# Two output projections as seven half-size products each, fewer idle products at the start, and one expert buffer refilled in two halves

## The chip, the core and the metric

The kernel runs on one core of a Trainium2 chip, written by hand against the engines: PE (TensorE, matmuls), DVE (VectorE), ACT (ScalarE), POOL (GpSimd) and SP, which here does nothing but issue DMAs. The engines run their own instruction streams and meet only at semaphores. The metric is the device time of one execution in microseconds (us). All data are fp32. One call of the matmul function in fp32 appears in the trace as two PE records (two passes), so a group of 8 calls is counted as x16 there; a transpose on PE is one record.

## The reference, cut to what matters

A transformer block for 256 tokens with 1024 features. Everything below is in the order in which the kernel does it; `rmsnorm` divides by a root mean square and multiplies by a gain.

```
h = rmsnorm(x, g_mix)
proj = h @ w_in                              # q, k, v, gates of two token mixers
merged = sigmoid(gate_a) * (y_a @ w_up_a) + sigmoid(gate_b) * (y_b @ w_up_b)
x = x + merged @ w_o_mix                     # first output projection, 256x1024 @ 1024x1024
q = rmsnorm(x, g_x) @ w_q_x                  # cross attention with 256 memory rows
x = x + attention(q, k, v) @ w_o_x           # second output projection, 256x1024 @ 1024x1024
logits = rmsnorm(x, g_ffn) @ w_router + b_router
# 32 experts, each token goes to its 4 best:
gu = xb @ w_gu[e] + b_gu[e]                  # 1024 x 2048 weights per expert
y = ((u + 1) * g * sigmoid(1.702 * g)) @ w_down[e] + b_down[e]      # 1024 x 1024 weights
out = rmsnorm(x + sum of gated y, g_final)
```

## The kernel before

**The two halves of the program.** The first part (to about 385 us) computes the mixers, the cross attention and the routing for all 256 tokens. The second part walks over the 32 experts; each has 64 slots for tokens, and its weights are six pieces of 2048 KB (`gu0` to `gu3`, `dn0`, `dn1`), which are read from HBM once and used once.

**Buffers.** `ring` has six slots of 2048 KB. All weights of the first part pass through it in the order of `PIECES`; the SP queue issues a piece as soon as the last PE group that reads the slot's old content has finished (`LAST_USE` names that group, `filled_of` waits for it). The experts' pieces of even experts go to `ring`; odd experts' first five pieces have buffers of their own (`r_odd0` to `r_odd3` and the end of `r_gbx`). In the first part these hold activations: `r_odd1` is `r_tp` (scratch, 1024 KB) and `hT` (1024 KB), `r_odd0` the cross-attention operands and the values. So the odd buffers are loaded in halves, each as its old content dies. SP issues everything in the order in which its program is written, and a wait holds up all that stands behind it. Its last issues before the expert loop (`first_block`, `odd_piece`, `odd_half`) fetch experts 0 and 1; then come `even_heads(1)` and the steady loop, in which SP waits for each buffer's `freed` semaphore. PE raises `freed` after the eight matmul calls that read a `gu` piece.

**The projections.** `sga` holds merged^T and `oxT` the attention output^T (feature chunks of 128 on the partitions: 8 chunks x 256 tokens). The weights lie in two ring slots, `om0`/`ox0` with output columns 0 to 511 and `om1`/`ox1` with 512 to 1023. `project_and_turn` on PE runs four groups (`om0_0`, `om0_1`, `om1_0`, `om1_1`; in the second projection `ro...`): output half n and token tile t, each 8 calls of 128x512 that accumulate over the chunks in one PSUM bank. DVE's `residual` adds each group to `x_tok` (`x_tok` = bank * scale + `x_tok`, one instruction of 128x512). After three groups the first half of x is complete, and PE turns it (8 transposes, `tx0`, `tx1`) ahead of the fourth group; the rest (`tx2`, `tx3`) follows when DVE has added the fourth. DVE's `gained` copies the turned x with its gain into `hT`, the operand of what comes next.

**Rows of the operand.** `begin(name)` waits until the bank that the name gets was drained of its previous user, `end(name)` marks it filled. Banks are dealt in turn over the list of `group_order()`.

**The start.** PE's `keep_busy(bank, n)` issues n products of the identity with itself, whose result nobody reads, in places where PE would be idle: 5 before the gain vector is turned, 4 before x is turned, 3 before the products `rb` that spread the norm's root over a row, and 8 behind `rb`, while ACT and DVE scale the turned x into `hT` for the q projection.

## Time and profile before

| | |
|---|---|
| median of 3 runs | 1299.54 us (1298.63 to 1300.12) |
| the profiled execution's own time, and its span | 1298.83 us, 1297.1 us |
| PE busy | 1244.9 us (96%) |
| DVE busy | 288.7 us (22%) |
| ACT busy | 145.3 us (11%) |
| moved by DMA | 454.70 MB, 351 GB/s over the span |
| mean granted TensorE clock | 0.991 |

The span is the time from the first to the last instruction. A busy PE means that PE had a matmul in flight, which says little by itself: the page's slices show PE busy nearly everywhere, and the DMA engines at 9 tenths or more and 425 to 429 GB/s from the fourteenth of forty slices on (a slice is 32.4 us) to the last but one. In the slices before them the DMA engines carry 85 to 401 GB/s.

### The profile page before, as it was taken

What the parts mean: (1) busy time and instruction counts of PE and PEld (TensorE: products, weight loads), DVE (VectorE), ACT (ScalarE), POOL (GpSimd) and SP (SyncE); (2) the same over time, 40 slices, a digit from 0 to 9 for tenths busy, and PEclk for the clock granted to TensorE, in tenths of its full rate; (3) what the DMA queues carried; (4) which work ended last, traced back from release to release, by engine and by line L of the source; (5) the groups of instructions that cost most, each with busy time, mean ns of one, the idle gap of its engine ahead of it and who ended that gap; (6) DMA issues with size and microseconds to landing.
All of it is one profiled execution on the core that took longest, in us unless ns stands there. A gap on an engine that the chain in (4) does not pass through costs nothing.

```text
span 1297.1 us, 14906 instructions
## 1 busy us (share of the span) xinstructions
PE 1244.9 (96%) x6197; PEld 614.1 (47%) x6197; DVE 288.7 (22%) x697; ACT 145.3 (11%) x325; POOL 8.2 (1%) x34
## 2 busy tenths in 40 slices
PE   9999999999999999999999999999989899999986
PEld 8868886757644343333343333443333344333322
DVE  2362234321132221111121111221111132211112
ACT  2223232101310000000000000000000000000001
POOL 1000000000000000000000000000000000000000
PEclk9999999999999999999999999999999999999998
DMA  9953233357559999999999999999999999999995
GB/s 332 318 194 110 85 131 113 115 195 268 203 195 401 428 428 427 426 427 428 429 429 428 428 429 429 427 428 428 428 428 428 428 428 427 427 427 428 427 425 238
DMA packets 60451, 454.70 MB, mean 351 GB/s; under 512 B 7228, under 2 KB 14072, under 8 KB 35064
## 3 DMA queue, kind: packets, MB, share of 16 engines
q1 hardware_dynamic: 58168, 452.49, 84.9%
q10 hardware_dynamic: 2240, 1.58, 0.4%
q8 instruction: 34, 0.56, 0.2%
q14 instruction: 9, 0.07, 0.0%
HBM read 453.00 MB, written 1.05 MB: 350 GB/s over the span
## 4 chain that ended last, share of the span: by engine, by line
PE 68%; DMA 29%; SPq 1%; issue 1%; DVE 1%; ACT 0%; POOL 0%; DVEq 0%; POOLq 0%; ACTq 0%
PE ps L1331 30%; DMA r_odd<-in_w_gu_dram 17%; PE ps L886 13%; DMA ring<-in_w_down_dram 11%; PE ps L893 7%; PE ps L1308 3%; PE ps L1324 3%; PE ps L1405 2%; PE ps L939 1%; PE ps L1103 1%; PE ps L1432 1%; SPq L494 1%; PE ps L1427 1%; PE ps L905 1%; PE ps L1252 1%
## 5 line engine op out<-in xcount | busy, mean ns | idle before, releaser
L1331 PE MATMUL ps<-r_odd,r_memT 128*64 128x512 f32 x1024 | 226.7, 597 | 15.3 <-DMA r_odd<-in_w_gu_dram 15.2
L1331 PE MATMUL ps<-ring,r_memT 128*64 128x512 f32 x1024 | 225.8, 594 | 11.9 <-DMA ring<-in_w_gu_dram 11.2
L1331 PE MATMUL ps<-ring,r_kx 128*64 128x512 f32 x768 | 176.9, 609 | 11.2 <-DMA ring<-in_w_down_dram 11.2
L1997 DVE TENSOR_SCALAR r_ga<-ps 128x512 f32<-128x512 f32 x32 | 22.1, 692 | 637.6 <-PE ps L1331 637.6
L1331 PEld LDWEIGHTS ps<-r_odd,r_memT 128*64 128x64 f32 x1024 | 73.4, 138 | 166.4 <-issue 137.2
L1331 PEld LDWEIGHTS ps<-ring,r_memT 128*64 128x64 f32 x1024 | 71.8, 137 | 160.2 <-issue 135.7
L886 PE MATMUL ps<-r_odd,ring 128*128 128x256 f32 x576 | 129.5, 383 | 0.0
L886 PEld LDWEIGHTS ps<-r_odd,ring 128*128 128x128 f32 x576 | 109.5, 192 | 18.0 <-issue 3.2
L1331 PEld LDWEIGHTS ps<-ring,r_kx 128*64 128x64 f32 x768 | 54.9, 140 | 130.0 <-issue 108.0
L827 ACT ACTIVATE r_ga<-r_ga 128x512 f32<-128x512 f32 x32 | 20.2, 630 | 462.8 <-DVE r_ga L1997 462.8
L1308 PE MATMUL ps<-r_dm,r_x 128*128 128x128 f32 x512 | 65.8, 282 | 0.0
L1324 PE MATMUL ps<-r_kx,r_dm 64*128 64x512 f32 x256 | 63.6, 615 | 0.7 <-ACT r_kx L833 0.7
L1308 PEld LDWEIGHTS ps<-r_dm,r_x 128*128 128x128 f32 x512 | 62.8, 197 | 1.6 <-DVE r_dm L1927 0.8
L1331 PE MATMUL ps<-r_gbx,r_kx 128*64 128x512 f32 x256 | 58.5, 598 | 0.8 <-DVE r_kx L2010 0.8
L833 ACT ACTIVATE r_kx<-ps 128x512 f32<-128x512 f32 x32 | 19.1, 597 | 333.9 <-PE ps L1331 333.9
L893 PE MATMUL ps<-ring,r_memT 128*128 128x512 f32 x112 | 49.2, 595 | 0.0
L1324 PEld LDWEIGHTS ps<-r_kx,r_dm 64*128 64x128 f32 x256 | 22.0, 186 | 41.3 <-issue 39.7
L1935 DVE TENSOR_TENSOR r_memT<-ps,sm 128x512 f32<-128x512 f32 x32 | 22.1, 692 | 64.6 <-PE ps L1308 64.6
L1331 PEld LDWEIGHTS ps<-r_gbx,r_kx 128*64 128x64 f32 x256 | 16.9, 136 | 40.6 <-issue 27.4
L1405 PE MATMUL ps<-r_ga,r_kx 32*64 32x512 f32 x256 | 35.8, 612 | 0.0
L893 PEld LDWEIGHTS ps<-ring,r_memT 128*128 128x128 f32 x112 | 21.0, 190 | 25.5 <-issue 25.2
L886 PE MATMUL ps<-r_memT,ring 128*128 128x256 f32 x128 | 28.6, 381 | 0.0
(342 smaller groups left out, 804.1 us busy)
## 6 DMA issues: line engine op xcount, KB each, us to landing
ring<-in_w_gu_dram SPq DMA_DIRECT2D x64, 2048.0 KB, 27.9
r_odd<-in_w_gu_dram SPq DMA_DIRECT2D x60, 2048.0 KB, 27.5
ring<-in_w_down_dram SPq DMA_DIRECT2D x47, 2048.0 KB, 22.6
r_gbx<-in_w_down_dram SPq DMA_DIRECT2D x15, 2048.0 KB, 30.2
ring<-in_w_in_dram SPq DMA_DIRECT2D x7, 2048.0 KB, 13.7
r_odd<-in_w_gu_dram SPq DMA_DIRECT2D x8, 1024.0 KB, 13.3
ring<-in_w_k_x_dram SPq DMA_DIRECT2D x2, 2048.0 KB, 9.5
ring<-in_w_v_x_dram SPq DMA_DIRECT2D x2, 2048.0 KB, 7.9
```

What stands on the lines that cost most here:

```text
L494: sp.dma_start(odd_slot[j], gu_dram[e, j] if j < 4 else dn_dram[e, j - 4]).then_inc(odd_loaded[j], 16)
L827: nc.scalar.activation(sig, gact, ACT.Sigmoid, scale=1.702).then_inc(sig_done, 1)
L833: nc.scalar.activation(y_slot, ps[:, ZBK, :], ACT.Copy).then_inc(yslot_ready, 1)
L886: last = mm(o[:, j * T:(j + 1) * T], w(k), src[:, k, :], start=(k == 0), stop=(k == kk - 1))
L893: last = mm(o, src[:, k, t * P:(t + 1) * P], w[:, k, 0:n], start=(k == 0), stop=(k == C - 1))
L905: mm(o[:, 0:P], ident[:], ident[:], start=True, stop=True)
L1308: last = mm(ps[:, buf, c * P:(c + 1) * P], x_rows[:, t, 2 * q + c // 2, c % 2], place[:, t], start=(t == 0), stop=(t == 1))
L1324: last = mm(ps[:, YB + 2 * t + n, :], scat[half, t * P:(t + 1) * P], y_slot[half, :], start=False, stop=False, skip_group_check=True)
L1331: last = mm(ps[n * SLOTS:(n + 1) * SLOTS, bk, :], stationary_, moving(n), start=start, stop=stop, skip_group_check=True)
L1405: mm(ps[n * SLOTS:(n + 1) * SLOTS, GBK + b, :], cur[q * NE:(q + 1) * NE, :], bgu_rows[q * NE:(q + 1) * NE, :], start=True, stop=False, ski ...
L1935: V.tensor_tensor(xg[:, buf, 4 * q:4 * q + 4], ps[:, bank_, :].rearrange("p (c s) -> p c s", c=4), gain_half[q], ALU.mult).then_inc(xg_rea ...
L1997: V.tensor_scalar(gact, ps[:, GBK, :], 7.0, None, ALU.min).then_inc(g_limited, 1)
```

## The change

There are three edits.

**1. Seven products.** Each projection is cut into halves of tokens (rows of the operand), of features (the sum) and of outputs (columns). With operand quarters a11 (tokens 0 to 127, chunks 0 to 3), a12 (tokens 0 to 127, chunks 4 to 7), a21, a22 and weight quarters b11 (chunks 0 to 3, outputs 0 to 511 of `w1`), b21, b12, b22, where `w1` is the slot of `om1`/`ox1` and `w2` that of `om0`/`ox0`, PE computes seven products P1 to P7 of 4 calls each (128x512) in the order of `SEVEN`: 1, 2, 3, 6, 7, 5, 4. DVE makes the sums that they need: four over the operand (128x512, written to `sums`, which is `r_tp`), and four over the weights (128x2048, written in place into the ring slots). DVE adds each product into all quarters of x that it belongs to (`ADDED_TO`: 12 additions of 128x512 in all, in place of 4). `sums_ready` tells PE and DVE how far the sums are.

**2. Idle products.** `keep_busy` is called with 2, 1, 2 and 6 in place of 5, 4, 3 and 8.

**3. First refill in halves.** The first refill of the `gu0` buffer (with the piece of expert 2) is issued as two DMAs of 1024 KB: the first half after PE's first four calls of expert 0 (`first_half_freed`), the second after all eight.

SP's order changes with edit 1: the slot of `om0`/`ox0` is free after P5 and that of `om1`/`ox1` after P4, and the half of `r_odd1` that is `r_tp` is loaded after P5 of the second projection.

```
-            "vx1": "vx3", "ua": "ua3", "ub": "ua3", "om0": "om0_1", "om1": "om1_1", "qx0": "qx1", "qx1": "qx3",
-            "ox0": "ro0_1", "ox1": "ro1_1"}
+            "vx1": "vx3", "ua": "ua3", "ub": "ua3", "om0": "omP5", "om1": "omP4", "qx0": "qx1", "qx1": "qx3",
+            "ox0": "roP5", "ox1": "roP4"}
...
+SEVEN = (1, 2, 3, 6, 7, 5, 4)
+ADDED_TO = {1: ((0, 1), (0, 0), (1, 0), (1, 1)), 2: ((0, 1),), 3: ((0, 0),), 6: ((0, 0), (1, 0), (1, 1)),
+            7: ((1, 0), (1, 1)), 5: ((0, 0), (1, 0)), 4: ((1, 1),)}
...
+            first_block(range(4, 5))
+            filled_of(sp, "roP5")
             odd_half(1, 1, 0)
-            first_block(range(4, 6))
+            first_block(range(5, 6))
...
-            even_heads(1)
+            sp.wait_ge(first_half_freed, 1)
+            sp.dma_start(rows2[:, 0], gu_dram[2, 0][:, 0]).then_inc(first_half_loaded, 16)
+            sp.wait_ge(freed[s], 1)
+            sp.dma_start(rows2[:, 1], gu_dram[2, 0][:, 1]).then_inc(loaded[s], 16)
+            even_heads(1, range(1, HEADS))
...
+                weights(f"{piece_name}1")
+                product(1, upper_left, w1[:, 0:4])
+                product(2, upper_right, w1[:, 4:8])
+                weights(f"{piece_name}0")
+                pe.wait_ge(sums_ready, 5 * turn + 1)
+                product(3, lambda k: sums[:, 3, k], w2[:, 4:8])
+                pe.wait_ge(sums_ready, 5 * turn + 3)
+                product(6, lambda k: sums[:, 1, k], w1[:, 0:4])
+                product(7, lambda k: sums[:, 2, k], w2[:, 0:4])
+                pe.wait_ge(sums_ready, 5 * turn + 4)
+                product(5, lambda k: sums[:, 0, k], w2[:, 4:8])
+                pe.wait_ge(sums_ready, 5 * turn + 5)
+                product(4, lambda k: src[:, 4 + k, P:2 * P], w1[:, 4:8], range(2))
+                drained_of(pe, f"{prefix}P5")
                 transpose4(f"{turned}0", x_tok, 0)
                 transpose4(f"{turned}1", x_tok, 1)
+                product(4, lambda k: src[:, 4 + k, P:2 * P], w1[:, 4:8], range(2, 4))
...
+                link(V.tensor_tensor(sums[:, 0], a21, a22, ALU.add))
+                V.tensor_tensor(sums[:, 2], a11, a21, ALU.subtract)
+                link(V.tensor_tensor(sums[:, 1], sums[:, 0], a11, ALU.subtract))
+                V.tensor_tensor(sums[:, 3], a12, sums[:, 1], ALU.subtract).then_inc(sums_ready, 1)
...
+                V.tensor_tensor(b12, b22, b12, ALU.subtract).then_inc(sums_ready, 1)
...
+                V.tensor_tensor(b11, b12, b11, ALU.add).then_inc(sums_ready, 1)
+                dve.wait_ge(sums_ready, 5 * turn + 3)
+                product_added(1)
+                product_added(2)
+                filled_of(dve, f"{prefix}P3")
+                V.tensor_tensor(b22, b22, b11, ALU.subtract).then_inc(sums_ready, 1)
+                product_added(3)
+                product_added(6)
+                V.tensor_tensor(b21, b21, b11, ALU.subtract).then_inc(sums_ready, 1)
+                product_added(7)
+                product_added(5)
                 gained(f"{turned}0", hT, g0, 0)
                 gained(f"{turned}1", hT, g0, 1)
+                product_added(4)
```

On PE, the first projection stood like this before (`r_ga` is the operand, `ring` the weights, `ps` a bank, the brackets hold the semaphores waited for; `drainedN` is bank N):

```order
L893 MATMUL ps<-ring,r_ga 128x512 [waits merged_ready,drained6,loaded4]
L893 MATMUL ps<-ring,r_ga 128x512 [waits merged_ready] x7
L893 MATMUL ps<-ring,r_ga 128x512 [waits merged_ready,drained7,loaded4]
L893 MATMUL ps<-ring,r_ga 128x512 [waits merged_ready] x7
L893 MATMUL ps<-ring,r_ga 128x512 [waits merged_ready,drained0,loaded5]
L893 MATMUL ps<-ring,r_ga 128x512 [waits merged_ready] x7
L875 MATMUL ps<-ident,r_x 128x128 [waits drained1,drained7,drained6]
L875 MATMUL ps<-ident,r_x 128x128 x3
L875 MATMUL ps<-ident,r_x 128x128 [waits drained2]
L875 MATMUL ps<-ident,r_x 128x128 x3
L893 MATMUL ps<-ring,r_ga 128x512 [waits merged_ready,drained3,loaded5]
L893 MATMUL ps<-ring,r_ga 128x512 [waits merged_ready] x7
```

Now it stands like this from the third product on (ahead of it are P1 and P2, 4 calls each on `r_ga`; `r_odd1` holds the operand sums):

```order
L1218 MATMUL ps<-ring,r_odd1 128x512 [waits drained1,sums_ready]
L1218 MATMUL ps<-ring,r_odd1 128x512 x3
L1218 MATMUL ps<-ring,r_odd1 128x512 [waits drained2]
L1218 MATMUL ps<-ring,r_odd1 128x512 x3
L1218 MATMUL ps<-ring,r_odd1 128x512 [waits drained3,sums_ready]
L1218 MATMUL ps<-ring,r_odd1 128x512 x3
L1218 MATMUL ps<-ring,r_ga 128x512 [waits drained4,sums_ready]
L1218 MATMUL ps<-ring,r_ga 128x512
L891 MATMUL ps<-ident,r_x 128x128 [waits drained5,drained3]
L891 MATMUL ps<-ident,r_x 128x128 x3
L891 MATMUL ps<-ident,r_x 128x128 [waits drained6]
L891 MATMUL ps<-ident,r_x 128x128 x3
```

Two calls of P4 stand ahead of the 8 transposes and two behind them, and the transposes wait for bank 3, P5's. Three of the seven products wait for `sums_ready` by themselves, and P6's wait covers P7.

On DVE, the same projection before (`ps` to `r_x` is one addition into x, `ps,vT` one turned pair of chunks):

```order
L1833 SCALAR_TENSOR_TENSOR r_x<-ps,r_x 128x512 [waits filled6,x_again]
L1833 SCALAR_TENSOR_TENSOR r_x<-ps,r_x 128x512 [waits filled7]
L1833 SCALAR_TENSOR_TENSOR r_x<-ps,r_x 128x512 [waits filled0]
L1569 TENSOR_TENSOR r_odd1<-ps,vT 128x512 [waits filled1]
L1569 TENSOR_TENSOR r_odd1<-ps,vT 128x512 [waits filled2]
L1833 SCALAR_TENSOR_TENSOR r_x<-ps,r_x 128x512 [waits filled3]
L1569 TENSOR_TENSOR r_odd1<-ps,vT 128x512 [waits filled4]
L1569 TENSOR_TENSOR r_odd1<-ps,vT 128x512 [waits filled5]
```

Now, from the third operand sum on (the first two stand ahead of it; `ring<-ring` is a sum over weights):

```order
L1887 TENSOR_TENSOR r_odd1<-r_odd1,r_ga 128x512
L1888 TENSOR_TENSOR r_odd1<-r_ga,r_odd1 128x512 [waits v_chain]
L1891 TENSOR_TENSOR ring<-ring 128x2048 [waits loaded5,loaded4]
L1894 TENSOR_TENSOR ring<-ring 128x2048 [waits filled6,sums_ready]
L1881 SCALAR_TENSOR_TENSOR r_x<-ps,r_x 128x512 [waits filled6,sums_ready]
L1881 SCALAR_TENSOR_TENSOR r_x<-ps,r_x 128x512 x3
L1881 SCALAR_TENSOR_TENSOR r_x<-ps,r_x 128x512 [waits filled7,drained6]
L1899 TENSOR_TENSOR ring<-ring 128x2048 [waits filled0,drained7]
L1881 SCALAR_TENSOR_TENSOR r_x<-ps,r_x 128x512 [waits filled0]
L1881 SCALAR_TENSOR_TENSOR r_x<-ps,r_x 128x512 [waits filled1,drained0]
L1881 SCALAR_TENSOR_TENSOR r_x<-ps,r_x 128x512 x2
L1902 TENSOR_TENSOR ring<-ring 128x2048 [waits drained1]
```

The first weight sums stand ahead of every addition, and P1 is added four times before the sum for P5 is made.

On SP, the last issues before the expert loop were these (`filledN` is bank N filled by PE, `freedN` a ring slot that PE has finished with):

```order
L491 DMA r_odd0<-in_w_gu_dram 128x2048 [waits filled5]
L491 DMA r_odd1<-in_w_gu_dram 128x2048
L483 DMA ring<-in_w_down_dram 128x4096 [waits filled7]
L483 DMA ring<-in_w_down_dram 128x4096 [waits filled3]
L491 DMA r_odd2<-in_w_gu_dram 128x2048 [waits sq_done]
L491 DMA r_odd1<-in_w_gu_dram 128x2048 [waits filled5]
L483 DMA ring<-in_w_gu_dram 128x4096 [waits freed4]
L483 DMA ring<-in_w_gu_dram 128x4096 [waits freed5]
```

Now they are these:

```order
L500 DMA r_odd0<-in_w_gu_dram 128x2048 [waits filled0]
L492 DMA ring<-in_w_down_dram 128x4096 [waits filled6]
L500 DMA r_odd1<-in_w_gu_dram 128x2048 [waits filled6]
L492 DMA ring<-in_w_down_dram 128x4096 [waits filled7]
L500 DMA r_odd2<-in_w_gu_dram 128x2048 [waits sq_done]
L500 DMA r_odd1<-in_w_gu_dram 128x2048 [waits filled5]
L549 DMA ring<-in_w_gu_dram 128x2048 [waits first_half_freed]
L551 DMA ring<-in_w_gu_dram 128x2048 [waits freed4]
L492 DMA ring<-in_w_gu_dram 128x4096 [waits freed5]
```

The half of `r_odd1` has moved behind the first `dn` piece and its wait, and the first refill is two rows in place of one.

## Rows read from the trace of the kernel before

**Rows 1.** Waits of PE, whole span: waiter, releaser, us in total, times, longest.

```profile
PE ps L1331 <- DMA r_odd<-in_w_gu_dram: 15.2, 11, 2.3
PE ps L1331 <- DMA ring<-in_w_down_dram: 11.2, 6, 2.7
```

**Rows 2.** Windows: stretch, length, engines busy, PEclk, DMA share, GB/s (last).

```profile
383.00:384.00 1.00, 1.00 (x11) 0.88 (x11) 0.00 (x0) 0.00 (x0) 0.00 (x0) 1.00 0.06 25
389.50:390.00 0.50, 0.50 (x6) 0.50 (x6) 0.00 (x0) 0.00 (x0) 0.00 (x0) 1.00 2.48 459
...
395.50:396.00 0.50, 0.50 (x6) 0.14 (x2) 0.00 (x0) 0.00 (x0) 0.00 (x0) 1.00 1.51 393
600.00:1200.00 600.00, 572.51 (x2894) 221.05 (x2892) 112.18 (x258) 34.05 (x64) 0.00 (x0) 0.99 1.01 428
```

**Rows 3.** Chain of waits, second projection to first expert: start, us, what.

```profile
342.43 20.60 PE ps L893 x48
363.03 0.87 PE ps L875 x8
363.90 6.88 PE ps L893 x16
...
384.98 3.58 PE ps L1331 x16
388.57 2.08 PE ps L1308 x16
390.65 9.59 PE ps L1331 x43
```

**Rows 4.** Chain of waits, first projection.

```profile
269.33 20.60 PE ps L893 x48
```

**Rows 5.** Timeline of DVE around the first projection: start, us, instruction [idle before].

```profile
270.09 0.69 DVE L1826 TENSOR_TENSOR r_ga<-r_ga,r_gbx 128x512 f32<-128x512 f32 x1
...
290.57 1.28 DVE L1569 TENSOR_TENSOR r_odd<-ps,vT 128x512 f32<-128x512 f32 x2
```

**Rows 6.** Groups of DVE by form: line, operands, count, busy us, mean ns.

```profile
L1666 DVE TENSOR_TENSOR r_odd<-r_odd 128x1024 f32<-128x1024 f32 x1 | 1.2, 1226 | 0.0
```

**Rows 7.** Timeline of SP's DMA queue from the second projection on.

```profile
356.19 14.94 SPq L483 DMA_DIRECT2D ring<-in_w_down_dram  x2
...
388.61 12.86 SPq L483 DMA_DIRECT2D ring<-in_w_gu_dram  x4
```

**Rows 8.** DMA issues of the page: KB each, us from issue to landing.

```profile
ring<-in_w_gu_dram SPq DMA_DIRECT2D x64, 2048.0 KB, 27.9
```

**Rows 9.** Chain of waits, the first microseconds.

```profile
2.15 2.50 PE ps L905 x10
...
6.86 2.42 PE ps L918 x16
...
9.95 0.45 PE ps L926 x4
10.40 1.79 PE ps L905 x16
```

**Rows 10.** Timeline of the first microseconds, all engines.

```profile
4.12 1.06 ACT L679 ACTIVATE r_odd<-r_x 128x1024 f32<-128x1024 f32 x1 [1.20 <-DMA r_x<-in_x_dram]
...
4.58 0.27 PE L910 MATMUL ps<-ident,r_odd 8*128 8x8 f32 x1
...
5.46 1.23 DVE L1577 SCALAR_TENSOR_TENSOR r_odd<-r_x 128x1024 f32<-128x1024 f32 x1 [5.46 <-DMA r_x<-in_x_dram]
...
7.24 0.17 DVE L1585 RECIPROCAL sm<-sm 128x2 f32<-128x2 f32 x1 [0.27 <-ACT sm L681]
...
10.93 3.23 DVE L1591 SCALAR_TENSOR_TENSOR r_odd<-ps,vT,r_dm 128x256 f32<-128x256 f32 x8 [3.52 <-ACT r_dm L669]
...
12.02 13.98 PE L939 MATMUL ps<-r_odd,ring 128*128 128x256 f32 x64
```

**Rows 11.** Window of PE at the first gate projections: PE busy, PEclk, DMA, GB/s.

```profile
87.00:88.00 1.00, 1.00 (x3) 0.50 0.88 326
```

More of the change, by code:

```diff
@@ L107, in group_order @@
         g += [f"ub{n}", f"ua{n}"]
[L108 removed]
+    g += [f"omP{n}" for n in SEVEN] + ["tx0", "tx1", "tx2", "tx3"]
     g += ["qx0", "qx1", "sx0", "qx2", "sx1", "qx3", "sx2", "pt0", "sx3"]
@@ L112, in group_order @@
     g += [f"ox{HX - 1}"]
-    g += ["ro0_0", "ro0_1", "ro1_0", "tf0", "tf1", "ro1_1", "tf2", "tf3"]
+    g += [f"roP{n}" for n in SEVEN] + ["tf0", "tf1", "tf2", "tf3"]
     return g
@@ L255, in program @@
         wr = r_kx[:, 1536:1536 + C * NE].rearrange("p (c e) -> p c e", c=C)
+        sums = r_tp.rearrange("p (s k t) -> p s k t", s=4, k=4)
         nar4 = r_p[:, 512:768]
@@ L1193, in _, with project_and_turn, product, upper_left @@
                 end(f"ua{n}", feature_group(f"ua{n}", [stationary(w, 2 * n), stationary(w, 2 * n + 1)], yaT, PAIRS))
-            def token_group(prefix, piece_name, src, n, t, ready):
-                weights(f"{piece_name}{n}")
-                name = f"{prefix}{n}_{t}"
-                end(name, token_part(begin(name), wslot(f"{piece_name}{n}", C, 512), 512, src, t, ready))
-            def project_and_turn(prefix, piece_name, src, turned, ready):
-                token_group(prefix, piece_name, src, 0, 0, ready)
-                token_group(prefix, piece_name, src, 0, 1, ready)
-                token_group(prefix, piece_name, src, 1, 0, ready)
-                drained_of(pe, f"{prefix}0_0")
-                drained_of(pe, f"{prefix}0_1")
+            def project_and_turn(prefix, piece_name, src, turned, ready, turn):
+                w1, w2 = wslot(f"{piece_name}1", C, 512), wslot(f"{piece_name}0", C, 512)
+                def product(n, lhs, rhs, part=range(4)):
+                    o = begin(f"{prefix}P{n}") if part[0] == 0 else bank(f"{prefix}P{n}")
+                    for k in part:
+                        last = mm(o, lhs(k), rhs[:, k], start=(k == 0), stop=(k == 3), skip_group_check=True)
+                    if part[-1] == 3:
+                        end(f"{prefix}P{n}", last)
+                def upper_left(k):
+                    ready(k)
+                    return src[:, k, 0:P]
+                def upper_right(k):
+                    ready(4 + k)
+                    return src[:, 4 + k, 0:P]
+                weights(f"{piece_name}1")
[12 more added lines that the diff above has]
+                drained_of(pe, f"{prefix}P5")
@@ L1421, in gate_up @@
                                 last.then_inc(gate_done, 1)
+                        if is_block(i, 0) and kk == 0:
+                            last.then_inc(first_half_freed, 1)
                     last.then_inc(odd_freed[j] if odd and j < HEADS else freed[eslot[EXPERT_PIECES[j]]], 1)
@@ L1827, in _, with residual_and_turned, product_added @@
                     .then_inc(merged_ready, 1)
-            def residual(prefix, n, t, scale):
-                name = f"{prefix}{n}_{t}"
-                filled_of(dve, name)
-                xv = x_tok[:, t, n * 512:(n + 1) * 512]
-                drain(name, V.scalar_tensor_tensor(out=xv, in0=bank(name), scalar=scale, in1=xv, op0=ALU.mult,
-                                                   op1=ALU.add))
-            def residual_and_turned(prefix, scale, turned, g0):
-                for n, t in ((0, 0), (0, 1), (1, 0)):
-                    residual(prefix, n, t, scale)
+            def residual_and_turned(prefix, piece_name, src, scale, turned, g0, turn):
+                w1, w2 = wslot(f"{piece_name}1", C, 512), wslot(f"{piece_name}0", C, 512)
+                b11, b21, b12, b22 = w1[:, 0:4], w1[:, 4:8], w2[:, 0:4], w2[:, 4:8]
+                a11, a12, a21, a22 = (src[:, k:k + 4, t:t + P] for t in (0, P) for k in (0, 4))
+                def product_added(n):
+                    name = f"{prefix}P{n}"
+                    filled_of(dve, name)
+                    for t, half in ADDED_TO[n]:
+                        xv = x_tok[:, t, half * 512:(half + 1) * 512]
+                        last = V.scalar_tensor_tensor(out=xv, in0=bank(name), scalar=scale, in1=xv, op0=ALU.mult, op1=ALU.add)
+                    drain(name, last)
+                    drained_of(dve, name)
+                link(V.tensor_tensor(sums[:, 0], a21, a22, ALU.add))
+                V.tensor_tensor(sums[:, 2], a11, a21, ALU.subtract)
+                link(V.tensor_tensor(sums[:, 1], sums[:, 0], a11, ALU.subtract))
+                V.tensor_tensor(sums[:, 3], a12, sums[:, 1], ALU.subtract).then_inc(sums_ready, 1)
+                for slot in (f"{piece_name}0", f"{piece_name}1"):
+                    dve.wait_ge(loaded[slot_of[slot]], need[slot])
+                V.tensor_tensor(b12, b22, b12, ALU.subtract).then_inc(sums_ready, 1)
+                dve.wait_ge(sums_ready, 5 * turn + 2)
+                filled_of(dve, f"{prefix}P1")
+                V.tensor_tensor(b11, b12, b11, ALU.add).then_inc(sums_ready, 1)
[9 more added lines that the diff above has]
+                product_added(5)
```

32 lines of the change are left out of this document (18 added, 14 removed).

## The prediction

> **What bounds the kernel now.** I read PE's waits first. The two largest are for weights of experts, 26.4 us over 17 waits, and the third of PE's rows is of the same kind [rows 1]. From 600 to 1200 us the DMA engines are full at 428 GB/s while PE is busy 572.5 of 600 us [rows 2]. So in the expert part the stream of weights sets the end. Its length is fixed by bytes, and what can move the end is when the stream starts without a gap.
>
> Then the windows around its start. At 383 to 384 us the engines are almost idle (25 GB/s): experts 0 and 1 have been fetched as far as buffers allow. SP's next issue, at 388.61 us, is the first refill [rows 7], and data flow from 389.5 us [rows 2]. It is released by the first eight calls of expert 0 (sixteen records, 3.58 us, from 384.98 us) [rows 3]. So the stream starts when PE gets there, and DMA had been idle for some 6 us before.
>
> Last, the chain of waits over the first part: it is PE nearly throughout. The projections stand in it whole: 48 records in 20.60 us, 8 transposes in 0.87 us, 16 records in 6.88 us [rows 3], and the same 20.60 us in the first projection [rows 4]. Hence a microsecond that PE saves before 385 us should come off the end, until the prefetch of experts 0 and 1 is no longer done in time.
>
> **The change part by part.**
>
> *Seven products, PE side.* One record of 128x512 takes 20.60/48 = 0.429 us, one call 0.858 us. A projection had 32 calls and now has 28. Four calls less are 3.43 us; two projections give **6.87 us**, if PE waits for nothing new. The transposes stay.
>
> *Seven products, DVE side.* This is what could take it back. Prices: an addition or an operand sum of 128x512 takes 0.69 us [rows 5]. A weight sum is 128x2048 fp32 from two tensors in SBUF. No row shows that size; 128x1024 takes 1.226 us [rows 6], so each 512 columns above the first 512 add 0.534 us, and 2048 columns take 2.29 us. Independent instructions of 128x512 overlap: two took 1.28 us [rows 5], so 0.6 us each but the last; for one that waits for another I add 0.05 us. The bound from below is this 2.29 us; from above I take four instructions of 128x512, 2.77 us. I take 2.29, since the size step is read from the same operation.
>
> Clock starts at P1 = 0 (269.33 us) [rows 4]. DVE has merged the last chunks at 270.09 + 0.69, that is 1.45. PE without waits ends P1, P2, P3, P6, P7, P5 at 3.4, 6.9, 10.3, 13.7, 17.2, 20.6 and half of P4 at 22.3.
> - Four operand sums: 4.3. PE wants them for P3 at 6.9.
> - Weight sums b12 and b11: 6.5 and 8.8. PE wants b11 for P6 at 10.3, a slack of 1.5.
> - P1 added four times, 11.4; P2 once, 12.1; b22, 14.5. P5 wants it at 17.2, a slack of 2.7.
> - P3 once, P6 three times, 17.1; b21, 19.4. P4 wants it at 20.6, a slack of 1.2.
> - P7 twice, 20.7; P5, filled at 20.7, twice, 22.05. The transposes want it at 22.3, a slack of 0.3.
>
> So PE never waits, and DVE, busy some 19 of the 22 us, is just not the bound. The tail behind P4 is as before: one addition, then two times four transposes. The x that DVE adds to was read again long before, since in the trace DVE's first addition waits for PE alone. With 2.77 us per weight sum the chain ends at 24.0 and the transposes lose 1.7 us per projection. In the second projection the operand is copied out by ACT instead of merged by DVE, 0.6 us behind PE's end, so DVE starts 0.8 us earlier against PE and the slacks grow by it.
>
> *DMA order.* P5's slot is released at 20.6 after the projection's start, P4's at 24.9; before, it was 13.8 and 28.4 (356.19 us is 13.8 behind 342.43) [rows 3, 7]. In the second projection this puts a 2048 KB piece and the 1024 KB half of `r_odd1` at 20.6, a piece at 24.9, and two more halves. That is 7.3 MB behind 20.6, at 428 GB/s 17.2 us, plus about 1 us from issue to first data (388.61 to 389.5) [rows 2, 7]: the engines are done at 38.8 and idle again. The first half refill is issued by the eight records (1.79 us) after PE starts expert 0, which stood at 384.98 - 342.43 = 42.55 and now at 39.1, so at 40.9. The prefetch is done with 2 us to spare, and the saving is passed on. Gaps of this kind ahead of the first projection are larger.
>
> *Refill in halves.* The first 1024 KB start 1.79 us earlier. But the next piece's buffer is released only at 390.65 + 3.58 = 394.2 us, since PE makes a gather between the two (2.08 us) [rows 3], and its data could flow from about 395.1 us. The first piece needs 4.9 us at full rate (2048 KB) [rows 8] and in fact filled 389.5 to about 395.5 us [rows 2]. So before, it overran the second piece's start by 0.4 us at most; finishing it earlier buys that and leaves a gap. Bounds 0 and 0.7 us; I take **0.2**.
>
> *Idle products.* PE starts at 2.15 us and its ten records take 2.50 us, 0.25 each, while the sixteen behind `rb` take 1.79, 0.112 each [rows 9]: TensorE runs at 1.2 GHz first and at 2.4 GHz later, and the transposes of x (16 in 2.42 us) [rows 9] hold the step; at 0.23 and 0.11 each it lies near 8.1 us. x's first tile is there at 4.12 us and its second at 5.46, the root at 7.41, while PE gets to the transposes at 6.86 and to `rb` at 9.95 [rows 9, 10]. So PE's idle products are late for x by 2 us. After the change: two products to 3.15, the gain's transpose (done at 4.58 before, its DMA unseen), one product, transposes from 4.12, eight at 0.23 to 6.0, eight to 7.8, two products to 8.5, `rb` (0.45 us) to 8.95 instead of 10.40. What follows (0.53 us of ACT to DVE's start at 10.93, 1.09 us to the q projection at 12.02) is the same, and six products (1.34 us) fit in it. Gain 1.45 us; if the gain vector lands only at 4.58 it is 0.75. I take **1.3**. From 12 us on PE is fed by weights that came earlier than it needs them, and waits for none up to the experts (its largest waits are those of [rows 1]).
>
> **Sum.** 6.87 + 0.2 + 1.3 = 8.4 us, against the profiled execution's 1298.83 us: 1290.4 us. That execution lies 0.7 us under the median of the three runs, so 1291 us on the median's scale (0.65% less). A difference of 0.2%, 2.6 us, is about what a measurement of this kernel can tell.
>
> **The rivals.**
>
> *A. Forecast*, PE's saving passes to the end: 1291 us. Chance 0.60. Its own range is 1289 (start 1.8, halves 0.7) to 1293.
>
> *B. The clock rises later.* Ahead of 8.1 us PE would now have done three idle products and mostly transposes, before it did nine. If the step comes only behind the q projection's start, transposes end at 7.8, two products at 8.8, `rb` at 9.7, six products at 0.5 us each at 12.7: q starts 0.7 us later than before, and each us of it at the lower level costs half. With 0 to 2.4 us of that the start loses 0.7 to 1.9 instead of gaining 1.3: 1293 to 1294.2 us. For it speaks that at 87 to 88 us the granted clock is 0.50 with PE busy 1.00 of 1.00 us [rows 11], so a busy PE alone does not settle it. Against it, that the step before came in the midst of transposes. Chance 0.17. The Trainium skill, TensorE: Matmul & The Clock Gate, Part 4: PE-mode transpose, says that transposes do not count as activity for the clock the way products do; by that rule this case is the likelier, and the time would be some 1293.5 us. The trace agrees only in part, since the clock there rose during transposes. The stretch at 87 us may shift as well, and each microsecond of it at the lower level is worth half of one, either way.
>
> *C. DVE is just too slow*: sums at 2.77 us, or 0.1 us more for each of its twenty instructions. PE then waits 1.7 us ahead of each pair of transposes: 1294.4 us. Chance 0.10.
>
> *D. Slower: weight sums crawl.* They read and write the ring slots from which PE streams at the same time, which nothing in the kernel before does. At twice the price (4.6 us each) PE waits 3.1 us at P6, 1.1 at P5, 3.8 at P4 and 1 at the transposes; each projection takes 33.9 us up to its last addition instead of 28.4, and the time is 1309 us. It decides from 1.1 us more per weight sum (3.4 instead of 2.3), where a projection loses what the start gains. DVE and PE do run side by side on SBUF all along at unchanged durations, which speaks against it. Chance 0.05.
>
> *E. The saving is not passed on*: the prefetch, now later in SP's order, is still running when the first refill is due. At 351 GB/s, the mean of the span, 7.3 MB take 20.9 us and end 1.6 us late; at 270 GB/s they end 7.9 us late: 1293 to 1299 us. Chance 0.08, as the engines hold 428 whenever they have work.
>
> The two edits beside the products may also do nothing: then 1292.5 us, inside A's range.
>
> **How the numbers follow.** A and B together hold 0.77; the range 1288.7 to 1295.5 takes in them and C. Faster by over 0.2% means under 1296.9: A, B, C and a little of E, 0.88. Within 0.2%: half of E and the edge of C, 0.07. Slower: D, 0.05.
>
> **What the profile after would show.** Right: 56 calls in place of 64 in the projections, each from P1 to the last addition in about 25 us; DVE's 128x2048 at 2.29 us; no wait of PE for DVE over 0.3 us in them; the q projection from about 10.7 us; SP's first refill at about 378.5 us with DMA idle ahead of it; the last record of PE 8.4 us earlier. Wrong would be a PE wait at P6 or the transposes (C, D), 0.25 us products behind `rb` (B), or DMA busy without a gap through 378 us (E).

## The result, and the profile after

| | before | after |
|---|---|---|
| median, range | 1299.28 us (1295.21 to 1300.12, 5 runs) | 1287.30 us (1286.96 to 1290.66, 5 runs) |
| profiled execution's own time, its span | 1298.83, 1297.1 us | 1287.77, 1286.0 us |
| mean granted clock | 0.991 | 0.995 |

The ratio is 0.9918, with a 95% interval of 0.9899 to 0.9938. The forecast was 1291.0 us, in a range of 1288.7 to 1295.5. So the change is faster, as forecast, but by 12 us where 8.4 were expected, and the time lies 1.4 us below the range. The spans differ by 11.1 us, and later runs of both kernels side by side (experiment 10) had medians 11.3 us apart, so some 0.7 us of the 12 is scatter between sets of runs. The rows of after that answer to the groups before the prediction show where the 11.1 us come from.

The chain of waits of after, first microseconds (start, us, what); [rows 9] are those of before:

```profile
0.78 3.83 DMA r_x<-in_x_dram
...
4.66 3.08 PE ps L934 x16
...
8.19 0.51 PE ps L942 x4
...
9.21 0.89 DVE r_odd L1632 x2
...
10.23 14.05 PE ps L955 x64
```

The norm's products (the x4 that ends at 8.70 us) start at 8.19 us, where it was 9.95 us, and the q projection at 10.23 instead of 12.19 us. In the chain stands x's DMA now, not PE's idle products.

The same view around the two projections and the first expert; [rows 3, 4] are those of before:

```profile
267.65 22.32 PE ps L1218 x52
289.97 0.87 PE ps L891 x8
290.84 1.73 PE ps L1218 x4
```

```profile
337.35 22.32 PE ps L1218 x52
...
376.47 3.58 PE ps L1368 x16
380.06 2.08 PE ps L1345 x16
```

52 records in 22.32 us are 0.429 us each, as before, so no wait lies among them. Records and transposes of a projection are 22.32 + 0.87 + 1.73 = 24.92 us, where they were 20.60 + 0.87 + 6.88 = 28.35: 3.43 us less in each.

DVE in the first projection (timeline; in brackets the idle time ahead), the answer to [rows 5, 6]:

```profile
269.21 0.69 DVE L1885 TENSOR_TENSOR r_odd<-r_ga 128x512 f32<-128x512 f32 x1
...
271.87 2.28 DVE L1891 TENSOR_TENSOR ring<-ring 128x2048 f32<-128x2048 f32 x1
274.19 2.29 DVE L1894 TENSOR_TENSOR ring<-ring 128x2048 f32<-128x2048 f32 x1
...
286.82 1.28 DVE L1881 SCALAR_TENSOR_TENSOR r_x<-ps,r_x 128x512 f32<-128x512 f32 x2
288.36 1.29 DVE L1881 SCALAR_TENSOR_TENSOR r_x<-ps,r_x 128x512 f32<-128x512 f32 x2 [0.26 <-PE ps L1218]
```

A weight sum of 128x2048 takes 2.28 to 2.29 us. From the first operand sum to the additions of P5 DVE is idle once, 0.26 us for PE's P5, and it is not late. It adds into x 14 times in each projection (5, 4, 2, 2 and 1 in its timeline), not 12 times as the section on the change says; the prediction's chain counts them rightly. PE's new rows in that section begin at P6, the fourth product (bank 1), and not at P3.

SP's queue and windows of after (PE busy, PEclk, DMA share and GB/s at the end), the answer to [rows 2, 7]:

```profile
378.38 0.33 SPq L549 DMA_DIRECT2D ring<-in_w_gu_dram  x1
380.10 0.33 SPq L551 DMA_DIRECT2D ring<-in_w_gu_dram  x1
385.76 7.19 SPq L492 DMA_DIRECT2D ring<-in_w_gu_dram  x3
400.31 3.76 SPq L492 DMA_DIRECT2D ring<-in_w_down_dram  x2
```

```profile
377.00:378.00 1.00, 1.00 (x8) 0.32 (x6) 0.00 (x0) 0.00 (x0) 0.00 (x0) 1.00 0.14 41
378.00:379.00 1.00, 1.00 (x6) 0.29 (x4) 0.00 (x0) 0.00 (x0) 0.00 (x0) 1.00 0.02 8
385.00:386.00 1.00, 1.00 (x8) 0.30 (x6) 0.00 (x0) 0.00 (x0) 0.00 (x0) 1.00 0.45 188
387.00:388.00 1.00, 1.00 (x8) 0.29 (x4) 0.00 (x0) 0.00 (x0) 0.00 (x0) 1.00 0.40 106
400.00:402.00 2.00, 2.00 (x12) 0.72 (x10) 0.00 (x0) 0.00 (x0) 0.00 (x0) 1.00 1.03 442
402.00:404.00 2.00, 2.00 (x12) 0.61 (x10) 0.00 (x0) 0.25 (x1) 0.00 (x0) 1.00 0.94 393
```

The first refill is issued at 378.38 us, behind a gap in which DMA moved 8 to 41 GB/s. A second gap lies at 385 to 388 us, ahead of the issue of gu1's refill at 385.76 us.

**The end.** SP's queue (timeline), and of the DMA view from 1275 us on the row of instruction fetches (packets, MB, share) and the output's issues (KB each, median us to landing), of after:

```profile
1281.40 2.51 SPq L602 DMA_DIRECT2D out_dram<-r_x  x4
```

```profile
q8 instruction: 1, 0.02, 0.3%
...
out_dram<-r_x SPq DMA_DIRECT2D x4, 256.0 KB, 2.0
```

and of a repeated run of the kernel before (experiment 1), whose end is the same as before's:

```profile
1287.42 3.80 SPq L585 DMA_DIRECT2D out_dram<-r_x  x4
```

```profile
q8 instruction: 2, 0.03, 0.7%
...
out_dram<-r_x SPq DMA_DIRECT2D x4, 256.0 KB, 3.2
```

The four output DMAs took SP 2.51 us after and 3.80 us before. In the trace three of them take 0.33 to 0.36 us each in both, and the fourth 0.33 us after and 1.63 us before. It also lands later. With the longer issue goes one more transfer of the kind "instruction", 16384 B, in the last 5 us.

**Where 11.1 us are.** Worked out from the two traces, each stretch from the start of one group to the start of the next, in us:

| stretch | before | after | gained | predicted |
|---|---|---|---|---|
| to the q projection | 12.19 | 10.23 | 1.96 | 1.3 |
| to P1 of the first projection | 257.14 | 257.42 | -0.28 | 0 |
| two projections, to the last addition | 28.38, 28.38 | 24.95, 24.95 | 6.86 | 6.87 |
| between them and on to expert 0 | 58.89 | 58.92 | -0.03 | 0 |
| expert 0 to the last scatter products | 901.79 | 901.18 | 0.61 | 0.2 |
| last scatter products to the end | 10.33 | 8.35 | 1.98 | 0 |

### The profile page after: what moved, and what is told of

Read it like the earlier page. It is cut to its first block, busy times and chain, and to the rows that moved or that the text cites. A ratio compares the mean times of both kernels' runs of the same rounds, so it can differ in the third digit from the quotient of the medians.

```text
span 1286.0 us, 14893 instructions
## 1 busy us (share of the span) xinstructions
PE 1233.1 (96%) x6163; PEld 607.7 (47%) x6163; DVE 324.7 (25%) x733; ACT 145.2 (11%) x325; POOL 8.0 (1%) x34
## 4 chain that ended last, share of the span: by engine, by line
PE 67%; DMA 30%; SPq 1%; DVE 1%; issue 1%; ACT 0%; DVEq 0%; ACTq 0%
PE ps L1368 30%; DMA r_odd<-in_w_gu_dram 18%; PE ps L902 13%; DMA ring<-in_w_down_dram 12%; PE ps L1218 4%; PE ps L909 3%; PE ps L1345 3%; PE ps L1361 3%; PE ps L1442 2%; PE ps L955 1%; PE ps L1119 1%; PE ps L1473 1%; SPq L503 1%; PE ps L1468 1%; PE ps L1289 1%
## 5 line engine op out<-in xcount | busy, mean ns | idle before, releaser
L1218 PE MATMUL ps<-ring,r_odd 128*128 128x512 f32 x64 | 27.8, 592 | 0.0
L902 PEld LDWEIGHTS ps<-r_memT,ring 128*128 128x128 f32 x128 | 24.0, 190 | 4.2 <-issue 1.0
## 6 DMA issues: line engine op xcount, KB each, us to landing
ring<-in_w_k_x_dram SPq DMA_DIRECT2D x2, 2048.0 KB, 10.6
```

What stands on the lines that cost most here:

```text
L902: last = mm(o[:, j * T:(j + 1) * T], w(k), src[:, k, :], start=(k == 0), stop=(k == kk - 1))
L1218: last = mm(o, lhs(k), rhs[:, k], start=(k == 0), stop=(k == 3), skip_group_check=True)
```

## The experiments

Each kernel was run with a profile and then in rounds against the kernel before. "The end" below is the last row of the table, from the start of the last scatter products to the end of the span. The first is a repeat, and the three behind it split the change into its edits.

**1. The kernel before once more.** No edit.

> The kernel before once more, for the spread. Theory T (tail by chance): in the two first profiles the program from the last matmul to the end took 8.3 us before and 6.4 us after, because the issue of the last output DMA took 1.63 us in the one and 0.36 in the other; if that is chance, this profile may show either, and the time is 1296 to 1300 us. Theory L (layout): the long issue belongs to the place of the instruction in SP's program, so it is there again at 1.6 us and the time is 1299 us.

1299.42 us (11 runs, 1295.71 to 1299.66), ratio 1.0004 (0.9996 to 1.0013). The profiled execution was one of the few near 1295: span 1294.0. The clock rose at 5.66 us instead of 8.12, the q projection began at 11.00 us, and the group of 64 records at 86 us took 14.01 us where before's took 15.38 with a fall of the clock in it. The spans differ by 3.1 us, of which these two make 2.6, and no edit made them. The end was 10.34 us, with the fourth issue at 1.63 us again.

**2. Only the start** (2, 1, 2, 6 in place of 5, 4, 3, 8).

```
-            keep_busy(bank("q1"), 5)
+            keep_busy(bank("q1"), 2)
...
```

> Only the counts of idle products (2, 1, 2, 6 in place of 5, 4, 3, 8). The start theory: q projection at 10.2 us, first expert at 383.3 us, 1.7 us less in all. Rival: the shift of the later fall of the clock (at 87 us) takes it back, 0 to 1 us less. If the tail theory L holds, the last issue is as long as before, since SP's program is the same; if T, it may be short.

1294.26 us (12 runs), ratio 0.9972 (0.9963 to 0.9981), some 4 us (2.5 to 4.8 by the ratio) where 1.3 were predicted for it. In the trace the q projection began at 10.19 us, 2.0 us earlier, and the end took 8.40 us, 1.9 us less. So an edit in the first 10 us took 2 us off the last 10. The two spans differ by 2.3 us only, since the stretch from expert 0 to the last scatter products took 903.10 us here and 901.79 in before. Theory L, as put for these first runs (the long issue belongs to its place in SP's program), fell: SP's program is the same, and the long issue is gone.

**3. Only the refill in halves.**

```
-            even_heads(1)
+            sp.wait_ge(first_half_freed, 1)
+            sp.dma_start(rows2[:, 0], gu_dram[2, 0][:, 0]).then_inc(first_half_loaded, 16)
...
```

> Only the first refill of gu0 in two halves. The sum of the prediction: 0.2 us less, bounds 0 and 0.7. Rival: the 0.6 us by which the expert stream gained beyond the start of expert 0 is this edit's, 0.6 us less. Under L the tail may be 1.3 us shorter too, since SP's program is one DMA longer; then 1.9 us less in all.

1299.06 us (11 runs), ratio 0.9999 (0.9990 to 1.0007). It is worth nothing that can be measured. The end was 10.33 us, so one DMA more in SP's program did not shorten it either.

**4. Only the seven products** (idle products 5, 4, 3, 8 as before, one refill).

> Only the seven products with the order of SP that belongs to them. PE theory: each projection 3.43 us less to its last addition (24.9 in place of 28.3), expert 0 at 378.1 us, and 6.9 us less in all, 1292.4 us. Rival: the products gave more than PE's four calls (for instance by SP's new order of prefetch), 8 us or more less. Under L the tail is as before or 1.3 us shorter, depending on the place.

1289.46 us (5 runs), ratio 0.9922 (0.9910 to 0.9935). From P1 of the first projection to expert 0 it took 108.83 us (270.28 to 379.11), where before took 115.65: 6.82 us less. The end took 8.39 us. Expert 0 came at 379.11 us and not at the 378.1 expected, since the clock fell for 6.8 us near 85 us, and the group of 64 records there took 16.34 us, 1 us more than before's 15.38.

After these the end was long (10.3 us) in three traces and short (8.4) in three, and the short ones were those with fewer calls in PE's stream. The next runs ask whether that is chance.

**5. Four calls fewer on PE.** The kernel before with 5, 4, 3, 4.

> The kernel before with 4 idle products in place of 8 behind the norm's products: PE's stream is 4 calls shorter, nothing else changes. Numbers so far: from the start of the last scatter products to the end of the span it took 10.33 to 10.34 us in three traces of kernels whose PE stream is as long as before, and 8.35 to 8.40 us in three whose stream is 8, 9 and 17 calls shorter; the fourth output DMA's issue took 1.63 to 1.70 us in the first and 0.36 us in the second. Theory L (where a fetch of instructions falls at the end depends on the length of PE's stream): with a boundary somewhere between 0 and 8 calls less, this run decides on which side of 4 calls it lies; with a short end the median is 2 us under the kernel before (1297.4), with a long one the same. Theory T (it is chance): either, and no tie to the length. Start: the q projection begins when DVE has its operand, so 4 idle products less cost nothing (12.2 us again) unless the clock falls or rises elsewhere.

1298.95 us (10 runs), ratio 1.0007 (0.9997 to 1.0018). The end was long, 9.87 us, with two fetches:

```profile
1291.39 3.37 SPq L585 DMA_DIRECT2D out_dram<-r_x  x4
```

```profile
q8 instruction: 2, 0.03, 0.5%
```

The q projection began at 11.32 us and not at the 12.2 expected, but expert 0 only at 386.05, 1.1 us later than in before: the clock fell for 6.8 us, and the group of 64 records near 86 us took 16.43 us.

**6. Idle products moved, not removed.** 2, 1, 2, 15, as many as before.

> The kernel before with its 20 idle products placed 2, 1, 2 and 15 in place of 5, 4, 3 and 8: PE's stream is as long as before, but x is turned as early as in the changed kernel. Theory L (length of PE's stream): the end is long again, 10.3 us, with the fourth output DMA's issue at 1.6 us. Theory T (chance): short or long. Theory of the start (PE was late for x): the norm's products come 1.5 us earlier; the 15 products then take 1.7 us in place of 0.7 for the 6 of the changed kernel, and the q projection begins at about 10.8 us instead of 10.2, which is 1.4 us before the 12.2 us of the kernel before. In all a gain of 1.4 us: 1298.0 us. If what helps is only that PE has fewer products in all, the q projection begins at 12 us and there is no gain.

1299.87 us (10 runs), ratio 1.0013 (1.0004 to 1.0023). The end was long, 10.26 us, as the length theory has it. The start's expectation was wrong. Its chain of waits:

```profile
4.69 3.40 PE ps L918 x16
...
8.98 3.35 PE ps L905 x30
12.33 13.82 PE ps L939 x64
```

x was turned as early as in the changed kernel, and the norm's products were done at 8.98 us. But 15 idle products are 30 records, 3.35 us (I had priced 15 records), and the q projection waits behind them until 12.33 us. What the idle products in front of x win can be lost behind `rb`. Here too the clock fell for 6.8 us, and the group near 86 us took 16.50 us.

**7. A longer PE stream.** The changed kernel with 160 waits that are long fulfilled.

```
+            for _ in range(160):
+                pe.wait_ge(consts, 1)
             four_blocks(6, 0)
```

> The changed kernel with 160 waits on a semaphore that was raised in the first 2 us, ahead of the block of expert 24 in PE's stream: 80 instructions more, which puts the length of PE's stream above that of the kernel before (in instructions, at four for each fp32 matmul call, the changed kernel has 64 less). Nothing is computed differently. Theory L: the end becomes long, 10.3 us in place of 8.35, the fourth output DMA's issue 1.6 us in place of 0.36, and the median is about 2 us over that of the changed kernel, 1289.3. Theory T: the end stays as it falls out, with no tie to the length. Rival: the waits themselves cost time. They stand where PE has about 5 per cent of slack against the stream of weights; at 0.05 us each they take 4 us there, which that slack would absorb; if not, the last expert moves by up to 4 us and the end stays at 8.35.

1288.83 us (4 runs), ratio 0.9928 (0.9911 to 0.9945), 1.5 us over the changed kernel's 1287.30, where 2 were expected. PE was held 4.7 us at the waits, but the stretch from expert 0 to the last scatter products took 901.68 us, 0.5 more than in after. The end took 10.52 us, 2.2 more. Expert 0 had begun 1.3 us earlier than in after, as the clock did not fall near 86 us. SP's queue and the DMA queues there:

```profile
1280.63 4.02 SPq L602 DMA_DIRECT2D out_dram<-r_x  x4
```

```profile
q8 instruction: 2, 0.03, 0.7%
...
out_dram<-r_x SPq DMA_DIRECT2D x4, 256.0 KB, 3.4
```

The second fetch and the long issue are back, with nothing added but instructions of PE.

**8. Seven calls fewer on PE.** The kernel before with 5, 4, 3, 1, three calls less than experiment 5.

> The kernel before with one idle product behind the norm's products in place of 8: PE's stream is 7 calls (28 instructions) shorter than before, as short as that of the kernel with the seven products alone. With 16 instructions less the end was still long (9.9 us, two instruction fetches), with 28 less by other means it was 8.4 us with one. Theory L (length of PE's stream): the end is 8.4 us here, the fourth output DMA's issue 0.36 us. Without it: 9.9 to 10.3 us. Start: DVE's operand sets the q projection, as with 4 idle products (11.3 us), not the idle products (12.2 us before). The median would be 1 us for the start and 2 us for the end under the kernel before, 1295.5 us; if the clock falls or rises later for want of products, the start loses up to 1 us.

1296.70 us (10 runs), ratio 0.9987 (0.9974 to 0.9999). The end took 8.42 us, with one fetch:

```profile
1291.34 2.50 SPq L585 DMA_DIRECT2D out_dram<-r_x  x4
```

```profile
q8 instruction: 1, 0.02, 0.3%
```

So the end is as theory L has it. The q projection began at 11.28 us, set by DVE's operand (11.32 in experiment 5). The median is 1.6 us under the kernel before's in these rounds (1298.31), and not the 3 us expected: the clock fell for 6.8 us again, the group near 86 us took 16.39 us, and expert 0 began at 386.00 us.

**9. DVE's margin.** The changed kernel with three more operand sums on DVE.

```
+                for _ in range(3):
+                    link(V.tensor_tensor(sums[:, 0], a21, a22, ALU.add))
                 link(V.tensor_tensor(sums[:, 0], a21, a22, ALU.add))
```

> The changed kernel with three more sums of 128x512 on DVE ahead of the first operand sum of each projection, each waiting for the one before: 3 x 0.65 = 2 us more work for DVE ahead of everything it does there. The prediction gave slacks of 1.5 us at P6, 2.7 at P5, 1.2 at P4 and 0.3 at the transposes. If these were right, PE now waits 0.5 us at P6, in all 0.8 at P4 and in all 1.7 at the transposes, in each projection: the projections take 26.6 us instead of 24.9, and the time is 3.4 us over the changed kernel's, some 1290.7. If DVE in truth had more room (1 us at the transposes), it is 2 us over. If the waits added up instead of taking each other's place (0.5 + 0.8 + 1.7 each), it would be 6 us over.

1290.63 us (4 runs), ratio 0.9944 (0.9926 to 0.9961). PE's waits in the first projection:

```profile
PE ps L1218 <- DVE ring L1896: 0.8, 1, 0.8
PE ps L891 <- DVE r_x L1881: 0.5, 1, 0.5
```

The three sums took 2.14 us. From P1 to the transposes the first projection took 24.16 us and the second 23.29, in place of 22.31. So the first lost 1.85 us of the 2.14, a margin of 0.3, and the second 0.98, a margin of 1.2. The prediction had 0.3 and 1.1. Behind these the waits took each other's place and did not add up. Together that is 2.8 us, where I had reckoned with 3.4 and left the second projection's extra margin out. That the median lies 3.3 us over the changed kernel's 1287.30, next to the 3.4, is in part luck.

**10. The changed kernel once more.** No edit.

> The changed kernel once more, beside the other three of this call. 1287.3 us (1287.0 to 1290.7) as before; the end from the last scatter products on 8.35 us, with one instruction fetch in it; the projections 22.3 us from P1 to the transposes. The q projection begins at 10.2 to 11.2 us, with the step of the granted clock (7.0 to 9.0 us in the three traces with these idle products).

1287.04 us (5 runs, 1286.37 to 1287.53), ratio 0.9917 (0.9903 to 0.9932). The clock rose at 8.75 us, the q projection began at 11.04, and the clock did not fall in the group near 86 us (14.01 us against after's 15.70). The end took 8.40 us.

**11. The second refill in halves too.**

```
+            for j in range(2):
+                s = eslot[f"gu{j}"]
...
+                sp.wait_ge(first_half_freed, j + 1)
+                sp.dma_start(rows2[:, 0], gu_dram[2, j][:, 0]).then_inc(half_loaded[j], 16)
...
-            even_heads(1, range(1, HEADS))
+            even_heads(1, range(2, HEADS))
```

> The changed kernel with the second refill (gu1 of expert 2) in two halves like the first. In its trace DMA moved 426 GB/s up to 377 us, 8 to 131 at 378 to 380, and again only 188, 254, 106 and 262 at 385 to 389, ahead of the issue of gu1's refill at 385.76 us; from 389 on it is full. Theory G (the last gap sets the start of the stream, and the first refill in halves gave nothing because this gap stays behind it): the first half of gu1's refill is now issued 1.79 us earlier, at 383.97 us, the data of 385 to 389 are about 0.9 MB more, and the end comes up to 1.8 us earlier: 1285.6 us. Theory N (the end is not tied to these bytes, or the next buffer, free 3.6 us later, makes a gap of its own): nothing, 1287.3 us.

1287.44 us (5 runs), ratio 0.9917 (0.9903 to 0.9931): no gain over experiment 10. The gap did close. Windows of the same stretches as above:

```profile
385.00:386.00 1.00, 1.00 (x6) 0.29 (x4) 0.00 (x0) 0.00 (x0) 0.00 (x0) 1.00 1.03 385
387.00:388.00 1.00, 1.00 (x8) 0.34 (x6) 0.00 (x0) 0.00 (x0) 0.00 (x0) 1.00 1.05 426
400.00:402.00 2.00, 2.00 (x12) 0.69 (x10) 0.00 (x0) 0.00 (x0) 0.00 (x0) 1.00 1.03 360
402.00:404.00 2.00, 2.00 (x12) 0.60 (x10) 0.00 (x0) 0.18 (x1) 0.00 (x0) 1.00 0.88 344
```

At 385 to 388 us DMA now moves 385 to 426 GB/s where it moved 106 to 188. But at 400 to 404 it moves 360 and 344, where after has 442 and 393: the lead ends at the next buffers, which SP refills at 400.38 us, as before at 400.31, when PE is done with them. Counted over SP's queue from the start of expert 0, 378.1 MB were left after 12 us against after's 378.9, and 371.2 in both after 30 us. Theory G fell, and N holds.

**12. No idle products at all.** The changed kernel with 0, 0, 0, 0.

> The changed kernel with no idle products at all. Up to 7.9 us PE then does one transpose of the gain and the 16 records that turn x. Theory B (the clock rises later for want of products): the granted clock rises behind 9.0 us, the latest of the traces so far, the transposes of x take 3.7 us in place of 3.1, and the q projection, 64 records of 0.22 us, loses half a microsecond for each one at the lower clock: it begins at 10.5 and ends up to 2 us later than in the changed kernel, 1289 us. Theory A (idle products do nothing for the clock's step): it rises between 5.7 and 9.0 us as in all the traces so far, the norm's products begin 0.3 us earlier with the root, and the q projection at 9.9 to 10.9 us: 1287.0 us.

1285.33 us (4 runs, 1284.98 to 1287.49), ratio 0.9910 (0.9892 to 0.9928). The chain of waits at the start:

```profile
4.58 3.65 PE ps L934 x16
8.23 0.47 PE ps L942 x4
...
9.21 0.89 DVE r_odd L1632 x2
...
10.23 14.05 PE ps L955 x64
```

The clock rose at 8.07 us, inside the 5.66 to 9.04 of all other traces, and the q projection began at 10.23 us. Theory B fell in this trace, and the median is 3.7 us under the 1289 that it gave. Of all kernels here this had the lowest median, 1.7 us under that of experiment 10, which ran beside it. 0.8 us of that is the start (10.23 against 11.04), and 0.8 the stretch from expert 0 to the last scatter products (900.21 against 901.01). Neither trace has a fall of the clock near 86 us. With 4 and 5 runs whose ranges overlap, the two are not told apart.

## Why the prediction was right, and where it failed

**The step that failed is the sum's silent assumption that the saving passes to the end one for one, with nothing changed behind the experts' last products (a term of 0 without a reason).** Expert 0 did move by 384.98 - 376.47 = 8.51 us. A further 2.0 us came off the end: 1.29 us of SP's fourth issue and 0.7 us of its landing. Without them the median would have been 1289.3 us, inside the range. The end over PE's stream length, counted in the programs against the kernel before (an fp32 call is four instructions, two PE and two weight-load records):

| kernel | PE's stream | fetches of 16384 B from 1275 us on | the end, us |
|---|---|---|---|
| after_waits | +16 | 2 | 10.52 |
| before, before_again, halves_alone, moved | 0 | 2 | 10.33, 10.34, 10.33, 10.26 |
| last_four | -16 | 2 | 9.87 |
| seven_less, seven_alone | -28 | 1 | 8.42, 8.39 |
| start_alone | -36 | 1 | 8.40 |
| after, after_again, sums_more, gu1_halves | -64 (gu1_halves -63) | 1 | 8.35, 8.40, 8.37, 8.33 |
| no_idle | -107 | 1 | 8.35 |

Fourteen traces split without an exception, and two pairs that differ in PE's stream alone flip it: last_four and seven_less (12 instructions), after and after_waits (80). That the length of PE's stream decides is shown for these lengths, from +16 to -107; where the switch lies between -16 and -28, and whether it comes back further off, is not. The trace does not name the engine whose instructions are fetched. It does show how closely the issue is tied to the fetch. In all six traces with a second fetch, SP's fourth issue begins 0.14 to 0.45 us behind the start of the fetch and ends 0.37 to 0.38 us behind its end, and without a fetch this issue takes 0.33 us. So the issue stands until the fetch is over; in last_four, where the fetch took 0.95 us in place of 1.55 to 1.78, it took 1.19 us in place of 1.59 to 1.85. Why it stands is not shown. The Trainium skill, Runtime: NRT & Kernel Launch, Instruction fetch mechanics, says that instructions come in blocks of 16 KiB, 256 instructions, over the sequencer's own DMA queue, and that the cost of crossing into the next block is mostly hidden. The size agrees with the 16384 B here. That the cost is hidden does not hold at this place: the end took 2 us more with the second fetch in it (1.5 in last_four).

**The other terms.**
- *Seven products, PE side*, 6.87 us: measured 6.86. Right.
- *Seven products, DVE side*: weight sums at 2.28 to 2.29 us for 2.29, transposes 22.32 us behind P1 for 22.3, no wait of PE up to there. The margins that the sum gave, 0.3 and 1.1 us at the transposes, came out as 0.3 and 1.2 in experiment 9. Rivals C and D did not happen. C's distance was small: 0.3 us more on DVE would have begun to cost time.
- *Idle products*, 1.3 us: measured 1.96 in after against before, mechanism right. Over all traces it is 1.1: with 2, 1, 2 and 6 the q projection began at 10.19 to 11.20 us (six traces, mean 10.6), with 5, 4, 3 and 8 at 11.00 to 12.29 (four, mean 11.7). The gain vector did not hold PE up (its transpose ran at 3.30 us), `rb` began at 8.19 us for the 8.5 expected. And the eight idle products behind `rb` had themselves held the q projection: with them it began 2.24 us behind `rb`'s start (12.19 - 9.95), without them 2.04 (10.23 - 8.19). Since the start moves by about 1 us between executions (10.23 and 11.04 for the changed kernel, 12.19 and 11.00 for the kernel before), 1.3 lies inside the scatter.
- *Clock* (rival B): with 2, 1 and 2 idle products ahead of `rb` it rose at 6.95 to 9.04 us in seven traces (mean 7.8), with 5, 4 and 3 at 5.66 to 8.34 in six (mean 7.1). Two executions of one kernel differ by more (7.00 and 8.75 in after and experiment 10), so a small part of B may be true, and the traces cannot tell it. Without any product (experiment 12) it rose at 8.07. The Trainium skill's rule (TensorE: Matmul & The Clock Gate, Part 4: PE-mode transpose), that transposes do not count as activity for the clock, would have it rise only behind them; here it rose at 8.07 us in the midst of 16 transposes that ended at 8.23, with nothing but transposes before.
- *Refill in halves*, 0.2 us: 0 within 0.1% (experiment 3). The mechanism was priced at the wrong place: the gap ahead of gu1's refill, which the prediction named, can be closed too without a gain (experiment 11). By the windows the lead is lost at the down buffers, which PE releases some 24 us after expert 0 starts.
- *DMA order* (rival E): the first refill was issued at 378.38 us for the 378.5 expected. The margin was smaller than said: data ran up to about 377 us, 1.4 us ahead of it and not 2. It did not matter.
- *From expert 0 on*, to the last scatter products: 900.2 to 901.7 us (median 901.18) in the seven traces with the seven products, 901.5 to 903.1 (median 901.71) in the seven without. The medians lie 0.5 us apart, but the ranges overlap, so that some of the 0.61 us goes with the change is likely and not shown. From what, no run tells; the refill in halves is not it, since seven_alone had 901.30 and halves_alone 902.18.

So the sum up to expert 0 was 8.17 us (the 0.2 of the refill come behind it) for 8.51 measured. That it is so close is in part luck of the two traces: the start gave 0.66 more than expected, and 0.31 was lost on the way. The step on the end was missing. The removed idle products act twice: on the start, which was priced at 1.3 us, and on the length of PE's stream, which was not priced; alone (experiment 2) they gave some 4 us. The seven products shorten the stream enough by themselves (experiment 4), so with both edits the 2 us come once.

## What to carry to other kernels

Where one engine is the chain up to some point, count its calls and multiply by the record's own duration: that was exact here. Then check the stretch behind the last matmul as a term of its own, with its DMA issues one by one, and look at the queue of kind "instruction" there: a few instructions more or less in a stream can bring a fetch into the last microseconds. Before a gap in the DMA stream is priced, look for the last buffer that a compute engine has to release; here, closing a gap ahead of that one bought nothing.

## What the runs showed of the hardware

- The end of the kernel took 9.9 to 10.5 us with a second instruction fetch of 16384 B in it and 8.3 to 8.4 us without, in 14 traces. An output DMA's issue that met the fetch ended 0.37 to 0.38 us behind the fetch's end, in all six.
- The time at which the granted clock rises scatters between 5.66 and 9.04 us. A fall near 85 to 87 us (3.4 or 6.8 us long) came in 9 of the 14 traces, in each of them 78.51 us behind the rise; the group of 64 records there took 14.01 us without one, 15.4 to 15.7 with the short one and 16.3 to 16.5 with the long one. The trace of the kernel before with the time of 1295.71 us had the earliest rise and no such fall, the one of 1298.83 us a rise 2.5 us later and a fall.
- 160 fulfilled waits, 80 instructions, held PE for 4.0 us more than the same place without them (4.7 against 0.7 us), 50 ns for each instruction, and the expert stretch took in all but 0.5 us of it.
